# A hybrid attention encoder on one core: row sums carried through the differential heads, keys projected earlier, weights subtracted on GpSimd

## The reference

```
q, k, v of 4 differential heads (2 maps of width 64 each), 8 latent heads (width 96, value 64)
# differential head, per block of 128 queries:
s = q @ k * scale - slope * |qpos - kpos|        # two maps m = 0, 1
p = softmax(s)
w = p[:, 0] - lam * p[:, 1]
o = w @ v
o = rmsnorm(o, g_sub, 1e-5) * (1 - lam_init)
# latent head: k, v from c_kv @ w_ukv, q from c_q @ w_uq, then softmax(q k) v
```

## Time and profile before

| | |
|---|---|
| median of three runs | 1219.01 us (1218.58 to 1220.04) |
| the profiled execution | 1218.42 us, of which its span 1216.1 us |
| mean granted TensorE clock | 0.997 of full |
| PE busy | 1191.5 us, 98% of the span |
| DVE / ACT / POOL busy | 892.4 / 601.8 / 541.8 us |
| attention steps 8 to 21 of layer 0 | 120.06 to 177.62 us |
| the same of layer 1 | 719.17 to 777.28 us |

### The profile page before, as it was taken

The page is one execution under the profiler, slowest core; times in us unless marked ns, Lnnn a source line. Parts: engine busy times, 40 slices in busy tenths (PEclk is TensorE's granted clock), DMA queues, the critical chain, the costliest instruction groups (busy, mean ns, idle before and its releaser), DMA issues.

```text
span 1216.1 us, 16360 instructions
## 1 busy us (share of the span) xinstructions
PE 1191.5 (98%) x5700; PEld 975.7 (80%) x5700; DVE 892.4 (73%) x1341; ACT 601.8 (49%) x986; POOL 541.8 (45%) x339
## 2 busy tenths in 40 slices
PE   8999889999999999999999999999999999999997
PEld 7877578888888888888888766788888888888886
DVE  4658967756778776879846688677658678767896
ACT  6345666744544344435423466676444444344443
POOL 1001344622865576556510023446047664766462
PEclk9999999999999999999999998999999999999999
DMA  6521101124234322430324211102252234223402
GB/s 192 138 55 61 45 18 35 53 87 153 75 86 137 115 87 85 130 111 30 104 66 112 61 37 43 36 18 85 73 172 87 78 113 139 86 72 120 139 7 98
DMA packets 128131, 104.55 MB, mean 86 GB/s; under 512 B 5514, under 2 KB 107956, under 8 KB 128052
## 3 DMA queue, kind: packets, MB, share of 16 engines
q1 hardware_dynamic: 127840, 103.50, 28.4%
q10 hardware_dynamic: 84, 0.02, 0.0%
q0 software_dynamic: 128, 0.00, 0.0%
HBM read 99.84 MB, written 2.10 MB: 84 GB/s over the span
## 4 chain that ended last, share of the span: by engine, by line
PE 92%; DVE 4%; ACT 2%; issue 1%; DMA 1%; POOL 0%; SPq 0%; POOLq 0%; DVEq 0%; ACTq 0%
PE bank L1494 82%; PE bank L1561 3%; PE bank L1589 3%; PE bank L1533 2%; DVE pt_lo L1112 1%; PE bank L1508 1%; PE bank L1724 1%; DVE e_t L1092 1%; DMA xin<-in_x 1%; ACT pt_hi L770 0%; DVE k_pack L1158 0%; PE bank L1519 0%; PE bank L1669 0%; DVE v_pack L1151 0%; DVE e_t L1080 0%
## 5 line engine op out<-in xcount | busy, mean ns | idle before, releaser
L1494 PE MATMUL bank<-u_hi,w_hi 128*128 128x512 f32 x760 | 299.4, 394 | 0.3
L1494 PE MATMUL bank<-u_hi,w_lo 128*128 128x512 f32 x760 | 296.1, 390 | 0.0
L1494 PE MATMUL bank<-u_lo,w_hi 128*128 128x512 f32 x760 | 295.8, 389 | 0.0
L738 ACT ACTIVATE w_hi<-stage 128x1024 fp32r<-128x1024 f32 (+3 forms) x141 | 136.4, 976 | 221.0 <-DMA stage<-in_w_up 91.3
L1050 DVE TENSOR_TENSOR w_lo<-stage,w_hi 128x1024 fp32r<-128x1024 f32 (+2 forms) x116 | 134.8, 1171 | 59.8 <-ACT w_hi L738 59.3
L1494 PEld LDWEIGHTS bank<-u_hi,w_hi 128*128 128x128 f32 x760 | 142.7, 188 | 30.8 <-issue 2.5
L1494 PEld LDWEIGHTS bank<-u_hi,w_lo 128*128 128x128 f32 x760 | 142.6, 188 | 30.2
L1494 PEld LDWEIGHTS bank<-u_lo,w_hi 128*128 128x128 f32 x760 | 142.8, 188 | 28.6
L738 ACT ACTIVATE w_hi<-b 128x1024 fp32r<-128x1024 f32 x84 | 88.9, 1059 | 131.8 <-PE bank L1494 105.2
L1494 PE MATMUL bank<-w_hi,quad_hi 128*128 128x512 f32 x392 | 152.6, 389 | 0.0
L1494 PE MATMUL bank<-w_hi,quad_lo 128*128 128x512 f32 x392 | 152.5, 389 | 0.0
(11 more groups left out here) (233 smaller groups left out, 2263.4 us busy)
## 6 DMA issues: line engine op xcount, KB each, us to landing
stage<-in_w_up SPq DMA_DIRECT2D x64, 512.0 KB, 4.0
b<-in_w_down SPq DMA_DIRECT2D x56, 512.0 KB, 3.4
stage<-in_w_in SPq DMA_DIRECT2D x32, 512.0 KB, 3.9
stage<-in_w_out SPq DMA_DIRECT2D x16, 512.0 KB, 3.6
stage<-in_w_down SPq DMA_DIRECT2D x8, 512.0 KB, 3.4
xin<-in_x SPq DMA_DIRECT2D x4, 512.0 KB, 6.7
stage<-in_w_ukv SPq DMA_DIRECT2D x4, 512.0 KB, 3.3
out<-yout SPq DMA_DIRECT2D x8, 256.0 KB, 2.3
```

The costliest lines, as they stand in the source:

```text
L738: last = nc.scalar.activation(hi(w_hi, s)[:, :, d:d + n], st(r)[:, :, f:f + n], ACT.Copy)
L1494: mm = nc.tensor.matmul(acc, a, b, start=first and t == 0 and m == 0, stop=last and t == len(terms) - 1 and m == 2)
```

## The change

**Row sums carried.** The weights of map 0 are no longer divided by their row sum. The row sums of map 0 go into a tile of their own, sum0; the factor of map 1 is lam * sum0 / rsum1, and the result e0 - factor * e1 is the old weights times sum0. The RMSNorm after the values takes that scale out, with its epsilon multiplied by sum0 squared (eps0). **Subtraction on POOL.** `weights` on DVE is gone; POOL multiplies e1 and then subtracts in place. **Order on DVE.** Both score readings stand ahead of `coef`. **Fillers.** v0, v1, kp0, q0, v2, v3, q1, q2 in steps 8 to 14 and 17; the ukv blocks are loaded ahead of the uq blocks; for v0 to v3, kp0 and kp1 (EARLY_LOW) ACT's high part stands ahead of the exps and DVE's low part one step earlier. **Column sums.** stat_c one step later, stat_b behind the score pair; the rope keys' low part one step later.

```diff
-    for use, n in (("q0", 9), ("v0", 10), ("kp0", 11), ("v1", 13), ("q1", 14), ("v2", 16), ("q2", 17), ("v3", 18)):
+    for use, n in (("v0", 8), ("v1", 9), ("kp0", 10), ("q0", 11), ("v2", 12), ("v3", 13), ("q1", 14), ("q2", 17)):
...
+EARLY_LOW = ["v0", "v1", "v2", "v3", "kp0", "kp1"]
...
-BLOCKS += [("uq", 0), ("uq", 1), ("ukv", 0), ("ukv", 1)]
+BLOCKS += [("ukv", 0), ("ukv", 1), ("uq", 0), ("uq", 1)]
...
-                nc.gpsimd.tensor_scalar(e_slot(t), e_slot(t), coefs[:, t:t + 1], cols(lam_b, 0, l), ALU.mult, ALU.mult
+                nc.gpsimd.tensor_scalar(e_slot(t), e_slot(t), coefs[:, t:t + 1], coefs[:, t - 1:t], ALU.mult, ALU.mult
                                         ).then_inc(t1_ready, 1)
+                pool.wait_ge(t1_ready, val(t1_ready, l, i + 1))
+                nc.gpsimd.tensor_tensor(e_slot(t - 1), e_slot(t - 1), e_slot(t), ALU.subtract).then_inc(w_ready, 1)
...
-                                     accum_out=rsum[:, t:t + 1]).then_inc(e_ready, 1)
+                                     accum_out=rsum[:, t:t + 1] if e % 2 else sum0_of(e // 2)).then_inc(e_ready, 1)
...
+                    for use in ended(n - 1):
+                        if use in EARLY_LOW:
+                            gen(l, use)
                     if n < DSTEPS:
                         exp_diff(l, 2 * n)
                         exp_diff(l, 2 * n + 1)
...
-                nc.vector.reciprocal(coefs[:, t:t + 2], rsum[:, t:t + 2]).then_inc(coef_ready, 1)
-
-            def weights(l, i):
-                t = 2 * (i % 3)
-                dve.wait_ge(t1_ready, val(t1_ready, l, i + 1))
-                nc.vector.scalar_tensor_tensor(out=e_slot(t), in0=e_slot(t), scalar=coefs[:, t:t + 1],
-                                               in1=e_slot(t + 1), op0=ALU.mult, op1=ALU.subtract
-                                               ).then_inc(w_ready, 1)
+                if i % TT == TT - 1:
+                    hd = slice(i // TT % 2 * TT, (i // TT % 2 + 1) * TT)
+                    nc.vector.scalar_tensor_tensor(out=eps0[:, hd], in0=sum0[:, hd], scalar=SUBLN_EPS, in1=sum0[:, hd],
+                                                   op0=ALU.mult, op1=ALU.mult)
+                nc.vector.tensor_scalar(coefs[:, t:t + 1], sum0_of(i), cols(lam_b, 0, l), None, ALU.mult)
+                nc.vector.reciprocal(coefs[:, t + 1:t + 2], rsum[:, t + 1:t + 2]).then_inc(coef_ready, 1)
...
-                    if 0 < n <= DSTEPS:
-                        coef(l, n - 1)
                     if n < DSTEPS:
                         ttr(l, 2 * n)
                         ttr(l, 2 * n + 1)
-                    elif n == DSTEPS:
-                        weights(l, n - 1)
+                    if 0 < n <= DSTEPS:
+                        coef(l, n - 1)
+                    if n == DSTEPS:
                         row_max(l, 0)
...
-                    if 0 < n < DSTEPS:
-                        weights(l, n - 1)
...
                     for use in ended(n - 2):
-                        if use[0] != "o":
+                        if use[0] != "o" and use not in EARLY_LOW:
                             gen_low(l, use)
                     for use in ended(n - 1):
-                        if use[0] not in "vk":
+                        if use in EARLY_LOW:
+                            gen_low(l, use)
+                        elif use[0] not in "vk":
                             gen(l, use)
...
-                    pe.wait_ge(krb_copied, val(krb_copied, l, 16 if hd < 2 else 48))
+                    if hd:
+                        pe.wait_ge(krb_copied, val(krb_copied, l, 16 if hd < 2 else 48))
...
+                    if r == 2 and 0 <= g < DIFF_HEADS:
+                        stat_c(l, MISC_AT[f"sub{g}_c"], tmp_s[:, 1, :])
+                    if r == 3 and 0 <= g < DIFF_HEADS:
+                        stat_b(l, MISC_AT[f"sub{g}_b"], 3 + g)
```

More of the change, by code:

```diff
@@ L296, in trunk @@
     coefs = place("coefs", [P, 6], F32)
+    sum0 = place("sum0", [P, 2 * TT], F32)
+    eps0 = place("eps0", [P, 2 * TT], F32)
     tabq = consts[:, C_TABQ:C_TABQ + SEQ]
@@ L442, in o_tile, with sum0_of @@
             return u_hi[:, n - DIFF_HEADS, :], u_low(n - DIFF_HEADS)
+        def sum0_of(i):
+            k = i % (2 * TT)
+            return sum0[:, k:k + 1]
         def d_keys(g):
@@ L923, in _ @@
                     for use in ended(n - 1):
-                        gen(l, use)
+                        if use not in EARLY_LOW:
+                            gen(l, use)
                     if r == 3 and 0 <= g < DIFF_HEADS:
@@ L1321, in _ @@
                         ttr(l, 2 * n + 1)
[L1322 to L1323 removed]
+                    if 0 < n <= DSTEPS:
+                        coef(l, n - 1)
+                    if n == DSTEPS:
                         row_max(l, 0)
[L1325 removed]
+                    elif DSTEPS < n <= STEPS:
                         inverse_sum(l, n - 1 - DSTEPS)
@@ L1331, in _ @@
                         pv_out(l, g)
-                    if r == 0 and 0 <= g < DIFF_HEADS:
-                        stat_col(l, MISC_AT[f"sub{g}_c"], 2 * DIFF_D, SUBLN_EPS)
-                    if 0 < n < DSTEPS:
-                        weights(l, n - 1)
+                    if n == DSTEPS - 3:
+                        dve.wait_ge(krb_hi_made, val(krb_hi_made, l, 1))
+                        nc.vector.tensor_tensor(k_pack[NOPE:P, 0, 1, :], krf[NOPE:P, :],
+                                                k_pack[NOPE:P, 0, 0, :].bitcast(F32), ALU.subtract
+                                                ).then_inc(krb_lo_made, 1)
                     if read_pt and not pt_first:
@@ L1339, in _ @@
                         o_low(l, g, o_tile(g))
-                    if n == DSTEPS - 4:
-                        dve.wait_ge(krb_hi_made, val(krb_hi_made, l, 1))
-                        nc.vector.tensor_tensor(k_pack[NOPE:P, 0, 1, :], krf[NOPE:P, :],
-                                                k_pack[NOPE:P, 0, 0, :].bitcast(F32), ALU.subtract
-                                                ).then_inc(krb_lo_made, 1)
                     for use in ended(n - 2):
-                        if use[0] != "o":
+                        if use[0] != "o" and use not in EARLY_LOW:
                             gen_low(l, use)
                     for use in ended(n - 1):
-                        if use[0] not in "vk":
+                        if use in EARLY_LOW:
+                            gen_low(l, use)
+                        elif use[0] not in "vk":
                             gen(l, use)
+                    if r == 0 and 0 <= g < DIFF_HEADS:
+                        dve.wait_ge(coef_ready, val(coef_ready, l, TT * g + TT))
+                        dve.wait_ge(misc_done, val(misc_done, l, MISC_AT[f"sub{g}_c"] + 1))
+                        nc.vector.scalar_tensor_tensor(out=rc[:, :], in0=MISC_BANK[:, 0:TT], scalar=1.0 / (2 * DIFF_D),
+                                                       in1=eps0[:, g % 2 * TT:(g % 2 + 1) * TT], op0=ALU.mult, op1=ALU.add
+                                                       ).then_inc(misc_free, 1)
                     if r == 1 and 0 <= g < DIFF_HEADS:
@@ L1767, in _ @@
                     g, r = divmod(n - TT - 2, TT)
-                    if r == 3 and 0 <= g < DIFF_HEADS:
-                        stat_b(l, MISC_AT[f"sub{g}_b"], 3 + g)
                     for use, part in FILL.get(n, []):
@@ L1775, in _ @@
                         else:
-                            if use == "q0":
+                            if use == "v0":
                                 pe.wait_ge(c_lo_made, val(c_lo_made, l, 2 * KC))
@@ L1792, in _ @@
                         scores(l, n + 2)
-                    if r == 1 and 0 <= g < DIFF_HEADS:
-                        stat_c(l, MISC_AT[f"sub{g}_c"], tmp_s[:, 1, :])
                 pe.wait_ge(sc_free, val(sc_free, l, 2 * DSTEPS + MSTEPS))
```

1 line of the change is left out of this document (removed).

## The result

| | before | changed |
|---|---|---|
| median | 1218.8 us (6 runs, 1218.32 to 1220.04) | 1226.07 us (6 runs, 1222.39 to 1229.16) |
| ratio | | 1.0055, 95% interval 1.0042 to 1.0068 |
| profiled execution | 1218.42 us | 1226.74 us, span 1224.3, mean granted clock 0.991 |

The account below looks back on a forecast made before the run. TensorE, busy 98%, was the bound, its waits costing 10.6 us a layer. New waits of 6.8 left 3.8 gained, 7.6 in two layers, less 0.6: 7.0 us. 1218.42 became 1211.4; the median, 0.6 above, 1212.0; range 1204 to 1221.

Parts of the forecast that it names:

- turn of step 0: TensorE's first turn in a layer: subtraction done at 93.4 us, wanted at 92.75, so 0.65 late.
- stretches at 1.2 GHz: Half clock: layer 1 had two stretches; other idle may bring or spare such stretches, up to 1 us.
- the table of new waits: Step-by-step list of TensorE's new waits in layer 0, summing to 6.8 us against 10.6 lost before.
- Part 3 of the prediction: Score readings ahead of the reciprocal: chain to a turn 3.96 us instead of 2.45, covered by 4.18 in steps 2 to 7.
- The turn of step 1: Second turn in a layer: subtraction ends at 98.85 us, wanted at 97.7, so 1.1 late.
- kp0 for v0's low part: Step 10: kp0's bank waits 1.35 us for v0's low part, behind dq3's split, which stands behind the subtraction.
- the turn in step 9: Turn 0.8 us late: power, t1, then a subtraction behind dq3's low part.
- the turns of steps 12 and 15: Turns late by 0.45 and 0.75 us, from the 3.96 us chain.
- four small ones: Steps 16 to 22: 0.8 us of new waits in all, in four small ones.
- Half clock in layer 0: Sign, named beforehand, that would make the prediction wrong; no size given.
- VectorE's 18 us less: Sign in the new trace: VectorE some 18 us less busy, 0.55 saved a step, as the weights leave it.
- My condition for slower: Rival, chance 0.14, about 1224 us: GpSimd's subtraction takes 2.15 us; decides from some 1.8.

Follow-up runs that it names:

- experiment 5: Changed kernel plus one wait per layer: in step 1 VectorE waits for GpSimd's multiplication of step 0 before its row of low parts and splits; 1226.56 us, ratio 1.0051.
- Experiment 6: Changed kernel plus 12 unread matmuls per layer, in TensorE's wait ahead of the first turn; 1224.43 us, ratio 1.0039.
- experiment 3: Changed kernel with the subtraction back on VectorE, score readings still ahead of the coefficients; 1229.05 us, ratio 1.0084.
- experiment 2: Changed kernel with the coefficients ahead of the score readings in all 16 steps, subtraction still on GpSimd; 1215.11 us, ratio 0.9967.
- experiment 10: The kernel of experiment 2 with the filler q2 in step 16 instead of 17; 1214.03 us, ratio 0.9958.
- experiment 9: The kernel of experiment 2 with v0's low part in step 9 ahead of dq3's low part and w_lo split; 1216.64 us, ratio 0.9972.

## Why the prediction was wrong

From 1212.0 to 1226.1 there are 14.1 us. Three terms, read from one execution of each kernel, make 13.8:

| per kernel | forecast | measured | missed by |
|---|---|---|---|
| turn of step 0, both layers | 2 x 0.65 late | 2 x 2.82 late | 4.3 |
| from there to step 25, full clock | 2 x 4.15 gained | 2 x 1.95 gained (99.53 to 97.58) | 4.4 |
| stretches at 1.2 GHz, against those before | 0, with "up to 1" in the range | 5.7 - 0.6 | 5.1 |

(4.15 is 10.6 - 5.05 - 1.1, less the allowance of 0.3.) That the sum lies so near the difference of medians is partly luck. The profiled execution of the change was 15.3 above the 1211.4 forecast for it, and of that another 1.4 stood ahead of the first late turn: its score pair of step 1 came at 93.23, that of before at 91.85.

**The step that failed** is in the table of new waits: "the reciprocal is done at 90.46, t1 runs to 91.33, and the subtraction meets the split". I had t1 at its median of 0.77 among VectorE's two-input instructions, without a reason, and let only the subtraction be held, though t1 reads SBUF as well. The view of L625 shows 2.62 there and experiment 5 shows 0.77 at once when the row is kept away. The rule of the Trainium skill that I cited (SBUF - State Buffer, "Who interferes with whom") makes no exception for an instruction with one input: it holds for any GpSimd instruction that reads SBUF. The trace agrees with the page, 2.62 against 0.77, and not with my use of it; that t1 stands through three instructions is more than the page says. Part 3 of the prediction looked for cover in steps 2 to 7 and found it; of step 0 it said nothing, and the table priced that turn at 0.65. There the cover was the whole head projection between the first two pairs: the reciprocal used to run at its start, and the new order moved it behind its end. Of a reordered instruction I asked how much longer its chain is (1.5 us) and not in whose company it now runs. The turn of step 1, forecast 1.1 late, waited for nothing in the changed kernel, and that of step 3, which was to fit, waited 0.51.

**The late steps** were right in kind and too low in size: kp0 for v0's low part 1.3 as forecast (1.35), the turn in step 9 0.94 (0.8), but the turns of steps 12 and 15 0.87 and 1.0 (0.45 and 0.75), and what I called "four small ones" of 0.8 together is 2.1: the column sum behind ScalarE's square, the spread behind the power, scores and values. On GpSimd the power now stands behind t1 and the subtraction. About 0.7 a layer of the gain that did not come is in no wait that I can name.

**The clock** I had as a small thing. Experiment 6 gives 1.4 us a stretch; the changed kernel's profiled execution had four in these steps, that of before two, which together cost it 0.6. How many an execution has varies, and the changed kernel's runs spread over 6.8 us with it (1222.39 at a mean granted clock of 0.996, 1229.16 at 0.990), those of before, in the same set, over 1.7. How much of the median is due to it is not measured. The windows give an estimate: at full clock throughout, the changed kernel would lose 2 x 2.82 and gain 2 x 1.95, so it would be 1.7 us slower. The profiled execution of experiment 6, which had no stretch, agrees: it is 4.1 above that of before (1222.50 and 1218.42), of which 2.45 stand ahead of the late turn (score pair of step 1 at 94.30 and 91.85). By this estimate the larger part of the 7.3 us between the medians is stretches at 1.2 GHz and the start of the execution (last section). That the new waits bring more of them is likely, and not shown. "Half clock in layer 0" was among the prediction's signs of being wrong, and it came.

**What was right:** the subtraction's 1.29, its effect when it meets w_lo (1.78 and 2.11), POOL's 41 us more (46.7). VectorE's 18 us less were 9.9, since its w_lo splits from the staging tiles and its low parts of dk and dq took 8.3 longer in sum (the groups of both kernels by form), which I put down to GpSimd's subtraction beside them. The prediction compared two different instructions when it called GpSimd 1.7 times as slow: a plain subtraction on VectorE measured 0.69 in experiment 3, and GpSimd's 1.29 is 1.9 times that. My condition for slower, a subtraction of over 1.8 us in general, was not met (1.29 in the middle; only the first of each layer took 2.11), and the kernel was slower all the same: that rival had the wrong mechanism. And the idea of the change was sound for its first part: with GpSimd subtracting and the coefficients left first, experiments 2 and 10 beat the kernel before by 4 to 5 us.

## What to carry to other kernels

When instructions change places, list for each what runs beside it in the new place, on the engine that shares its port with it, and not only what it waits for; above all at the head of a loop, where the steady state's cover is missing. Price an instruction on a shared port by its longest row and not by its median, when a queue of two-input instructions can stand beside it. A change made of several parts should be timed with each order or engine choice apart: here one part cost 11 us, stretches at 1.2 GHz included, and hid 4 us that the others gained. And if taking a wait away moves it to the next step (experiments 5 and 9), the engine behind it is full: start its input earlier, or take work from it.

## What the runs showed of the hardware

A GpSimd multiplication with one SBUF input waited through three VectorE instructions with two SBUF inputs (0.67, 1.22 and 0.68 us, back to back), and ended 2.61 after its start instead of 0.77. The GpSimd subtraction was let in after one: started at 94.67 beside dk_lo, it ended at 96.45 and held the w_lo of 95.22 until then (2.30 instead of 1.22). Why the two differ is open.

In the first 15 us of an execution the clock differs too: granted 1.00 in the window from 5 to 15 us of the kernel before, 0.66 in that of experiment 10. The granted clock does not show all of it: experiment 6 has 1.00 in that window as well, and yet its matmuls from 11.69 to 12.54 start 0.43 us apart, as they do in a stretch at 1.2 GHz, where those of before at 9.77 to 10.24 start 0.24 apart. Its score pair of step 1 came at 94.30, that of before at 91.85. The turn of step 0 came at 92.75 in the profiled execution of before and at 93.5 to 95.9 in those of the kernels that are not late there. So a profiled execution can lie 2.3 us above its kernel's median (experiment 10: 1216.36 and 1214.03), and positions in two traces were compared from the turn of step 0 on.
